# Two layers of a hybrid transformer block on one core: half norms in passes of four chunks without GpSimd, one modulation vector made at another place, attention's weight splits one tick later

## What is computed

```python
def ffn_sublayer(t, shift, scale, gate, g_pre, g_post, w_in, w_out):
    y = swiglu(modulate(rms_norm(t, g_pre), shift, scale), w_in, w_out)
    return t + FFN_RES * gate * rms_norm(y, g_post)
...
for l in range(DEPTH):
    mx = jnp.split(silu_c @ ada_w[l] + ada_b[l], N_MOD, axis=-1)      # nine vectors for the latent
    mc = jnp.split(silu_cc @ ada_w[l] + ada_b[l], N_MOD, axis=-1)     # nine for the context
    x = ffn_sublayer(x, mx[0], mx[1], mx[2], g[0], g[1], ffn_w_in[l, 0], ffn_w_out[l, 0])
    px = project(modulate(rms_norm(x, g[2]), mx[3], mx[4]), mix_w_in[l])
    ...
    ya, yb, yc = mix_latent(q_x, kv_x, kv_c, lam, win_sink[l], band_mask, key_valid)
    y = merge_branches(ya, yb, yc, px[9], diff_subln_g[l], lambda_init, branch_w[l], mix_w_out[l])
    x = x + mx[5] * rms_norm(y, g[3])
    x = ffn_sublayer(x, mx[6], mx[7], mx[8], g[4], g[5], ffn_w_in[l, 1], ffn_w_out[l, 1])
```

## Time and profile before

| | |
|---|---|
| median of three runs | 2966.91 us (2962.5 to 2967.18) |
| the profiled execution | 2961.36 us |
| its span in the trace | 2959.7 us |
| TensorE busy | 2786.3 us, 94%, 15738 matmuls |
| VectorE busy | 1755.1 us, 59% |
| ScalarE busy | 1254.7 us, 42% |
| GpSimd busy | 318.6 us, 11% |
| granted clock of TensorE, mean | 0.981 |
| read from HBM | 378.22 MB, 129 GB/s over the span |

### The profile page before, as it was taken

The page is one execution under the profiler, slowest core; times in us unless marked ns, Lnnn a source line. Parts: engine busy times, 40 slices in busy tenths (PEclk is TensorE's granted clock), DMA queues, the critical chain, the costliest instruction groups (busy, mean ns, idle before and its releaser), DMA issues.

```text
span 2959.7 us, 43176 instructions
## 1 busy us (share of the span) xinstructions
PE 2786.3 (94%) x15738; PEld 2308.4 (78%) x15738; DVE 1755.1 (59%) x2978; ACT 1254.7 (42%) x2275; POOL 318.6 (11%) x397
## 2 busy tenths in 40 slices
PE   6999999999899999998999989989999989999998
PEld 4888887876656676788888978767879766868897
DVE  5677366656645443367675376763667665545764
ACT  3222354336545434445222453222553555555443
POOL 0001021111200000022000030110211020001000
PEclk8999999999999999999999999989999999999999
DMA  5555356421111121145454445553554211324554
GB/s 237 165 197 197 93 159 213 142 86 36 44 36 36 51 82 58 50 157 164 164 191 150 132 158 186 186 175 105 153 184 144 70 65 58 118 79 157 213 172 134
DMA packets 106502, 384.46 MB, mean 130 GB/s; under 512 B 12273, under 2 KB 14065, under 8 KB 104177
## 3 DMA queue, kind: packets, MB, share of 16 engines
q1 hardware_dynamic: 86370, 303.82, 31.9%
q0 software_dynamic: 19984, 78.65, 8.0%
HBM read 378.22 MB, written 4.20 MB: 129 GB/s over the span
## 4 chain that ended last, share of the span: by engine, by line
PE 78%; DVE 10%; ACT 4%; issue 3%; POOL 2%; DMA 2%; SPq 0%; DVEq 0%; POOLq 0%; ACTq 0%
PE ps L1928 22%; PE ps L1920 21%; PE ps L1921 20%; PE ps L901 3%; PE ps L863 3%; PE ps L880 2%; DVE wlo L1483 2%; POOL acc L1036 2%; ACT whi L1174 1%; PE ps L853 1%; DVE work L1639 1%; PE ps L1981 1%; DVE mx L751 1%; PE ps L1984 1%; PE ps L1986 1%
## 5 line engine op out<-in xcount | busy, mean ns | idle before, releaser
L1483 DVE TENSOR_TENSOR wlo<-raw,whi 128x1024 fp32r<-128x1024 f32 x572 | 700.8, 1235 | 576.7 <-ACT whi L1174 576.1
L1920 PE MATMUL ps<-xhi,whi 128*128 128x512 f32 (+1 forms) x2432 | 829.4, 355 | 20.4 <-DVE xlo L1649 18.3
L1921 PE MATMUL ps<-xlo,whi 128*128 128x512 f32 (+1 forms) x2432 | 820.2, 351 | 0.0
L1174 ACT ACTIVATE whi<-raw 128x1024 fp32r<-128x1024 f32 x572 | 604.5, 1057 | 480.7 <-PE ps L1928 445.9
L1920 PEld LDWEIGHTS ps<-xhi,whi 128*128 128x128 f32 x2432 | 467.9, 192 | 90.9 <-DVE xlo L1649 20.8
L1928 PE MATMUL ps<-xhi,wlo 128*128 128x512 f32 (+1 forms) x2432 | 517.2, 356 | 15.5 <-DVE wlo L1483 15.5
L1921 PEld LDWEIGHTS ps<-xlo,whi 128*128 128x128 f32 x2432 | 468.2, 193 | 57.4
L1928 PEld LDWEIGHTS ps<-xhi,wlo 128*128 128x128 f32 x2432 | 406.8, 193 | 77.1 <-DVE wlo L1483 18.2
L1697 DVE SCALAR_TENSOR_TENSOR work<-ada,work 128x1024 f32<-128x1024 f32 x256 | 299.2, 1220 | 15.9 <-DMA ada<-in_ada_rows 15.9
L1920 PE MATMUL ps<-ghi,whi 128*128 128x256 f32 (+1 forms) x968 | 279.3, 314 | 16.0 <-ACT whi L1174 16.0
L1921 PE MATMUL ps<-glo,whi 128*128 128x256 f32 (+1 forms) x968 | 278.3, 315 | 0.0
(11 more groups left out here) (205 smaller groups left out, 3470.2 us busy)
## 6 DMA issues: line engine op xcount, KB each, us to landing
raw<-in_ffn_in SPq DMA_DIRECT2D x192, 512.0 KB, 4.8
ada<-in_ada_rows POOLq DMA_DIRECT2D x128, 512.0 KB, 4.4
raw<-in_merge SPq DMA_DIRECT2D x96, 512.0 KB, 3.6
raw<-in_ffn_out SPq DMA_DIRECT2D x88, 512.0 KB, 3.6
raw<-in_ffn_out SPq DMA_DIRECT2D x44, 384.0 KB, 3.2
raw<-in_v_a SPq DMA_DIRECT2D x32, 512.0 KB, 4.3
raw<-in_qk_a SPq DMA_DIRECT2D x32, 512.0 KB, 3.7
raw<-in_wo SPq DMA_DIRECT2D x24, 512.0 KB, 4.0
```

Of the source, the lines that this page charges most:

```text
L1174: act.activation(whi[:, g.ring(SPLIT), :], raw[:, g.ring(RAW), :], ACT.Copy).then_inc(hi_ready, 1)
L1483: dve.tensor_tensor(wlo[:, g.ring(SPLIT), :], raw[:, g.ring(RAW), :], whi[:, g.ring(SPLIT), :].bitcast(F32), ALU.subtract).then_inc(lo_rea ...
L1920: pe.matmul(o, w, hi[:, first + c, ph.span], start=start, stop=False)
L1921: pe.matmul(o, w, lo[:, first + c, ph.span], start=False, stop=False)
```

## The change

1. **Half norms.** The residual is made in two batches of four chunks: one gate pass and one add of 128x4x256 each. ScalarE squares four chunks in one pass into a new buffer `squares`, which lies where the `ada` ring is. VectorE sums squares, pairs against pairs, in three passes of 512 columns, and TensorE's second total takes the remaining two chunks in two products that accumulate. GpSimd has no part in it any more. The modulated activations are made in four slots of two chunks. TensorE's second total stands one slot earlier.
2. **One vector moves.** (1, 7) leaves the second layer's first `ffn_in` (four vectors are left) and is made in the second layer's key phase, one block per tile, behind the tile's rope. `SIDE_BLOCK` becomes functions of the phase.
3. **Attention.** The low split of the next group comes in a tile's second tick in place of its first, in the phases that are interleaved with attention.

```diff
+BATCHES = 2
...
-        adds = {"stat": 2, "inv": 2, "gated": KC, "x": KC, "xsq": KC, "xsum": KC - 1, "scaled": KC, "xhi": KC,
-                "xlo": KC}
+        adds = {"stat": 2, "inv": 2, "gated": BATCHES, "x": BATCHES, "xsq": BATCHES, "xsum": 3, "scaled": KC,
+                "xhi": KC, "xlo": KC}
...
-        (1, 0): [(1, 3), (1, 4), (1, 5), (1, 6), (1, 7)],
+        (1, 0): [(1, 3), (1, 4), (1, 5), (1, 6)],
...
-        add("rope", layer, src="qk_a", dst="k", first=8, tokens=T, iters=2, groups=4, tiles=4, adds={"rope": 8})
+        add("rope", layer, src="qk_a", dst="k", first=8, tokens=T, iters=2, groups=4, tiles=4,
+            side=range(KC) if last else (), vectors=[(1, 7)] if last else (), adds={"rope": 8, "made": int(last)})
...
+        squares = at("squares", [P, KC, S], 88 * KB)
...
+        def side_block(ph, made):
+
+            done_before = ada_order.index((ph.layer, 7)) * KC + ph.side[0]
+            every = ph.iters * ph.tiles // len(ph.side)
+            return done_before + made // every - 1 if made % every == 0 else None
...
-            def pool_norm(ph):
-
-                def add(c):
-                    pool.wait_ge(done["xsq"], base(ph, "xsq") + c + 1)
-                    if c == 1:
-                        pool.wait_ge(done["stat"], base(ph, "stat") + 1)
-                        first = tmp[:, 0, ph.span]
-                    else:
-                        pool.wait_ge(done["xsum"], base(ph, "xsum") + c - 1)
-                        first = acc[:, ph.span]
-                    pool.tensor_tensor(acc[:, ph.span], first, tmp[:, c % 2, ph.span], ALU.add)\
-                        .then_inc(done["xsum"], 1)
-
-                for chunks in ((), (), (1, 2), (3, 4, 5), (6, 7)):
-                    for c in chunks:
-                        add(c)
-                    yield
...
-                            if ph.side and j % 2 == 0:
-
-                                block = SIDE_BLOCK + ph.side[0] + (i * ph.tiles + j) // 2 - 1
-                                if block >= SIDE_BLOCK and block + ADA_RING < SIDE_BLOCK + KC:
-                                    pool.wait_ge(ada_dot, 2 * (block + 1))
-                                    load_ada(Idx(block + ADA_RING, 0, 0))
+                            block = side_block(ph, i * ph.tiles + j) if ph.side else None
+                            if block is not None and side_start(ph) <= block < side_start(ph) + KC - ADA_RING:
+
+                                pool.wait_ge(ada_dot, 2 * (block + 1))
+                                load_ada(Idx(block + ADA_RING, 0, 0))
...
-            def square(ph, c):
-
-                act.wait_ge(done["x"], residual(ph, c))
-                if c > 1:
-                    act.wait_ge(done["xsum"], base(ph, "xsum") + max(c - 2, 1))
-                act.activation(tmp[:, c % 2, ph.span], x[:, c, ph.span], ACT.Square).then_inc(done["xsq"], 1)
+            def square(ph, b):
+
+                act.wait_ge(done["x"], base(ph, "x") + b + 1)
+                act.activation(squares[:, 4 * b:4 * b + 4, :], batch(x, ph, b), ACT.Square).then_inc(done["xsq"], 1)
 
             def normed_high(ph, c):
 
...
                 inverse(HALF_STAT, ph.span, D, base(ph, "stat") + 1)
                 yield
                 yield
-                for chunks in ((0, 1, 2), (3, 4, 5), (6, 7)):
-                    for c in chunks:
-                        square(ph, c)
-                    yield
+                square(ph, 0)
+                yield
+                square(ph, 1)
+                yield
                 inverse(HALF_STAT, ph.span, D, base(ph, "stat") + 2)
                 yield
-                for chunks in ((0, 1), (2, 3, 4), (5, 6, 7)):
-                    for c in chunks:
-                        normed_high(ph, c)
+                for c in range(0, KC, 2):
+                    normed_high(ph, c)
+                    normed_high(ph, c + 1)
...
-                split_ahead(split_lo, ph, i, j)
-                yield
+                if not ph.overlapped:
+                    split_ahead(split_lo, ph, i, j)
+                yield
+                if ph.overlapped:
+                    split_ahead(split_lo, ph, i, j)
...
+            def residual_added(ph, b):
+
+                many = [P, KC // BATCHES, S]
+                dve.tensor_tensor(batch(work, ph, b), batch(work, ph, b),
+                                  inv[:, ph.span].unsqueeze(1).to_broadcast(many), ALU.mult).then_inc(done["gated"], 1)
+                dve.wait_ge(done["gated"], base(ph, "gated") + b + 1)
+                dve.tensor_tensor(batch(x, ph, b), batch(x, ph, b), batch(work, ph, b), ALU.add)\
+                   .then_inc(done["x"], 1)
+
+            def squares_summed(ph, b):
+
+                dve.wait_ge(done["xsq"], base(ph, "xsq") + b + 1)
+                first, second = squares[:, 4 * b:4 * b + 2, :], squares[:, 4 * b + 2:4 * b + 4, :]
+                dve.tensor_tensor(first, first, second, ALU.add).then_inc(done["xsum"], 1)
...
-                for chunks in ((0, 1, 2), (3, 4, 5), (6, 7)):
-                    for c in chunks:
-                        gated(ph, c)
-                    for c in chunks:
-                        added(ph, c)
+                residual_added(ph, 0)
+                yield
+                residual_added(ph, 1)
+                squares_summed(ph, 0)
+                yield
+                squares_summed(ph, 1)
+                dve.wait_ge(done["xsum"], base(ph, "xsum") + 2)
+                dve.tensor_tensor(squares[:, 0:2, :], squares[:, 0:2, :], squares[:, 4:6, :],
+                                  ALU.add).then_inc(done["xsum"], 1)
+                yield
+                newton(step, dve, base(ph, "inv") + 2, HALF_STAT, ph.span, D)
+                yield
+                for c in range(0, KC, 2):
+                    scaled(ph, c)
+                    scaled(ph, c + 1)
+                    normed_low(ph, c)
+                    normed_low(ph, c + 1)
...
-                            if ph.side and j % 2:
-                                ada_block(Idx(SIDE_BLOCK + ph.side[0] + (i * ph.tiles + j) // 2, 0, 0))
+                            block = side_block(ph, i * ph.tiles + j + 1) if ph.side else None
+                            if block is not None:
+                                ada_block(Idx(block, 0, 0))
...
-                def total(number):
-                    return pe.matmul(ps[:, HALF_STAT, ph.span], ones[:, :], acc[:, ph.span], start=True, stop=True)\
-                             .then_inc(done["stat"], 1)
+                def total(parts):
+                    for part in parts:
+                        last = pe.matmul(ps[:, HALF_STAT, ph.span], ones[:, :], part, start=part is parts[0],
+                                         stop=part is parts[-1])
+                    last.then_inc(done["stat"], 1)
 
                 pe.wait_ge(done["acc"], base(ph, "acc"))
                 pe.wait_ge(done["refined"], base(ph, "inv"))
                 wait(pe, done["yraw"], base(ph, "yraw"))
                 wait(pe, bank_free[HALF_STAT], ph.heads)
-                total(0)
-                for slot in range(10):
+                total([acc[:, ph.span]])
+                for slot in range(9):
                     yield
-                pe.wait_ge(done["xsum"], base(ph, "xsum") + KC - 1)
+                pe.wait_ge(done["xsum"], base(ph, "xsum") + 3)
                 pe.wait_ge(done["refined"], base(ph, "inv") + 1)
-                total(1)
-                for slot in range(3):
+                total([squares[:, c, :] for c in range(2)])
+                for slot in range(4):
```

31 lines of the change are left out of this document (11 added, 20 removed).

## The result

The changed kernel takes 2915.75 us (median of 4 runs, 2910.97 to 2916.9), the kernel before 2964.7 (4 runs, 2961.03 to 2967.18): ratio 0.9837, 95% interval 0.9824 to 0.9849, or 49.0 us less. 2913 was forecast, from a saving of 53.5 us.

What follows compares the result with a forecast made beforehand. TensorE, busy 94% of the span, was taken as the bound, so gains come where it stands still. 25.1 (vector) + 22.0 (half norms) + 7.0 (attention) - 0.6 (keys) = 53.5 us, from 2966.9 to 2913; eight-in-ten range 2893 to 2934.

Steps and rivals of the forecast that it cites:

- the third load can be issued only when the first block is used: Second layer's first ffn_in: six-block bodies stall on a ring of two; moving the vector saves 25.1 us, bounds 15 to 25.
- Moved vector, keys: Second layer's keys: one block per tile mostly fits VectorE's idle time; cost 0.6 us at kr, bounds 0 and 18.
- signs of being wrong: Ada wait in keys, wide passes over 1.8 us, whi waits over 1 us behind squares, low-split wait at a region's end.
- 2.4 us for the eight tiles: Keys: VectorE and GpSimd excluding each other would cost up to 0.3 us a tile; left out of the sum.
- forecast of 4.4: Half norm beside ffn_out: idle time falls from 6.8 us to 1.2 + 2.9 + 0.35; three halves save 7.2.
- the total is now two products: Half norm's total: two products of 256 columns where there was one; 0.35 us for the second.
- `wo` and the heads: Half norms at eight groups: 7.5 us saved for wo with the head behind it, 3.3 for the other head.
- the last pair, now behind the last product, gives some back: Beside wo and in the heads: loses part of what the earlier second total wins; no size of its own.
- A third of the chain's share of the splits: Attention: the later low split saves 7 us, bounds 0 and 15; splits hold 14.6 us of first layer's a, 6.6 of second's.
- the other four stretches give nothing: Attention: only a of each layer was counted for the later splits, the other four stretches as nothing.
- norms stay: Rival, chance 0.14: the ScalarE-VectorE hand-over, not GpSimd, sets the half norms; they give 8 us only, 2927 us.
- keys stall: Rival, chance 0.08: late loads of the moved vector stall the second layer's keys by 18 us, 2931 us.

Runs made afterwards that it cites:

- after_again: The changed kernel timed and profiled once more without any edit; 2915.26 us, ratio 0.9831.
- only_vector: The kernel before with the moved vector alone; 2937.37 us against 2964.01, ratio 0.9912.
- slot_later_everywhere_35: Changed kernel with xhi and xlo one slot later everywhere, 3 and 5 chunks around wo and heads, vector's broadcast and first loads ahead of queries; 2883.16 us, ratio 0.9736.
- slots_of_233: The changed kernel with the modulated activations made in slots of 2, 3 and 3 chunks as before; 2897.97 us in one run.
- the timed kernel: The kernel before with the later splits in attention alone; 2957.77 us, ratio 0.998, 6.2 us less.
- the better version: Changed kernel with xhi and xlo of a pair one slot later beside ffn_out and the values; 2897.03 us in one run, 2883.16 with further edits.

## Why the prediction came out right, step by step

**The total.** The time came out 2.3 us above the forecast of 2913.4. The saving was mis-sized by more, 49.0 us for 53.5: the forecast starts from a median of 2966.9, and the kernel before took 2964.7 beside the changed one, which hid 2.2 us of it. The part that is short is the half norms, 17.2 timed for 22.0; the vector gave 26.6 for 24.5, the splits 6.2 for 7.

**Moved vector, `ffn_in`: right in size, half right in cause.** The stage became the first layer's, 195.86 us. That the step "the third load can be issued only when the first block is used" is the whole cause is wrong: 5.7 of 25.1 are VectorE's own time.

**Moved vector, keys: right that it is small, wrong in place.** I expected the first block a microsecond late without TensorE seeing it, and 0.6 at `kr`. `kr` takes 7.4 us before and after. The wait for `ada` in the keys was one of its signs of being wrong. The cost is at the first block:

```profile
2227.19 1.22 DVE L1707 SCALAR_TENSOR_TENSOR work<-ada,work 128x1024 f32<-128x1024 f32 x1 [3.47 <-DMA ada<-in_ada_rows]
...
2228.34 1.75 DVE L1707 SCALAR_TENSOR_TENSOR work<-ada,work 128x1024 f32<-128x1024 f32 x1
```

The load was issued at 2217.85 and VectorE got it 9.3 us later, behind the broadcast, where 6.6 us had been estimated from one load and a half. VectorE waited 3.47 us, and TensorE 0.85 for the split behind it. Issued ahead of the queries, it costs nothing (keys 43.55).

The second dot there took 1.75 us instead of 1.22, beside a cosine of GpSimd that took 1.34, where undisturbed ones take 0.74. Of the 14 dots that start in the keys' window it is the only one lengthened, but the splits of the next three tiles are too:

```profile
2234.73 1.75 DVE L1473 TENSOR_TENSOR wlo<-raw,whi 128x1024 fp32r<-128x1024 f32 x1
...
2239.98 1.75 DVE L1473 TENSOR_TENSOR wlo<-raw,whi 128x1024 fp32r<-128x1024 f32 x1
...
2245.22 1.76 DVE L1473 TENSOR_TENSOR wlo<-raw,whi 128x1024 fp32r<-128x1024 f32 x1
```

The first of them starts 0.46 us after a cosine of 1.13 us began. In the kernel before, all eight splits of the keys take 1.22. The Trainium skill (SBUF — State Buffer, Who interferes with whom) has the two engines exclude each other in such a case; by it I had worked out 2.4 us for the eight tiles, and the trace shows 2.1 of VectorE's time, four passes at 0.53. TensorE waits for none of the three splits, so leaving the term out of the sum did no harm; the reason given for it, one undisturbed tile, was too little. `after_again` and `only_vector` have the same four passes; where the loads come ahead of the queries (`slot_later_everywhere_35`), none is lengthened.

**Half norms: 22.0 forecast, 17.4 found.** Beside `ffn_out` the parts are in their places, but two came out larger. The forecast of 4.4 is made of 4.1 of waiting and 0.35 for the total's second product, which TensorE spends working. The idle time is 4.56 us: 1.14 in the first half (1.2 was forecast), 3.3 at the pairs (2.9), 0.12 at the total. The wide pass took 1.22 us (1.2), the sums 0.68 (0.65), or 1.23 beside GpSimd's add for the other half. Mis-sized are the pairs, by 0.4, and the term for "the total is now two products": 0.35, and the stage's busy time grew by 0.55. So a half won 1.67 and not 2.4. The values won more (2.95 and 2.62 for 2.0). The step that failed is `wo` and the heads, 10.8 forecast and 6.8 found. That the second total comes 4 to 6 us earlier is right (4.9 at `wo`), and "the last pair, now behind the last product, gives some back" too, but it gives back over 3 us behind each of the two heads. With the old slots (`slots_of_233`) these five stretches take 136.8 us, 141.7 with the change, 148.6 before: the mis-sized term is the price of the four pairs.

**Attention: 7 forecast, 6.2 timed.** A third of the chain's share of the splits was a guess that came out well. That the other four stretches give nothing is wrong for the first layer's `b`, by 0.9 us. The 12.5 us between the two traces look like a larger gain, and the timed kernel does not bear them out; how much of the clock's part is the edit's stays open. Over all traces the first layer's `a` took 175.1 to 177.6 us with the old order (four traces) and 167.0 to 173.5 with the new one (ten), a mean gain of 6.4 with 4.0 of idle time, while the timed kernel gives at most 8.6 for all of attention.

Of the rivals, "norms stay" and "keys stall" did not come about; the hand-over between ScalarE and VectorE, the reason given for the first, is real, and was what the better version removed.

## What to carry to other kernels

Compare stages by three numbers at once: the length, the idle time of the bounding engine, and the granted clock. In attention idle time repeated and the length did not: it moved 6 us with the clock at like code. Beside `ffn_out`, where a chain on other engines sets the end, the length repeated and the idle time did not. A difference that only one of them shows, in one trace, is not yet an effect. An engine that waits on another in the middle of its in-order queue holds back what stands behind: put the work that nobody has to wait for (here the next weights' split) ahead of the hand-over, and let the hand-over lag one slot. Where a chain runs beside a fixed number of product groups, count what comes behind the last one; fewer, larger portions won over 3 us behind each head here, and beside the long stages the choice was worth at most 0.3 us.

## What the runs showed of the chip that I had not expected

- The granted clock falls in the same places, but not in every execution: with the new order and idle time at 15.6 to 15.7 us, the first layer's attention `a` ran at a mean clock of 0.94 to 0.99, mixtures of 2.4 and 1.2 GHz, and took 167 to 173.5 us in ten traces. The falls lie some 112, 156 and 170 us into the stage in most of them, and at each the clock was at 1.2 GHz for 6.8 us, for 3.4, or not at all, with the same waits of TensorE there (1.8, 1.6 and 3.3 us).
- At the same length of a stage, 40.8 us, TensorE was idle for 6.8 us at a clock of 1.00 and for 5.6 at 0.96.
- In three stages of 40 us with a longest wait of 1.87 us the clock fell for 3.4 us (0.96), with a longest wait of 1.22 it did not (1.00); but neither did it in the first of these stages of the kernel before, with one of 2.05.
- Four VectorE passes of 128x1024 in the keys took 1.75 us in place of 1.22, each behind the start of a cosine of GpSimd that was not done; where VectorE's pass had begun first, the cosine took up to 1.69 in place of 0.74.
- A load of 512 KB issued right behind a broadcast landed after 9.3 us, where the median is 4.4; in two other traces with the same order it took 9.0 and 9.4.
